# Second mixer of a hybrid encoder: three pieces of queue order moved (keys' output transfers, the last state update, the second band scores)

## The chip, the cores and the metric

The kernel runs on one core of a Trainium2 chip. It is one program in which the five queues (TensorE, VectorE, ScalarE, GpSimd, and SyncE, which issues the weight loads) are written out by hand and meet only through semaphores. The metric is the device time of the whole program in microseconds (us); lower is better. Below, PE is TensorE's matmul side, DVE VectorE, ACT ScalarE, POOL GpSimd.

## What is computed

The reference is a two-layer encoder trunk for 512 prompt tokens and 32 sample tokens that share the weights (544 columns, D_MODEL 1024). Each layer is half a SwiGLU, a mixer, half a SwiGLU. The change lies in the mixer of the second layer, which joins band attention (C) and a Mamba-2 state-space part (D):

```python
bq, bk, bv, z, xbc, dt = jnp.split(h @ w_in, [o1, o2, o3, o4, o5], axis=-1)
bo = band_prompt(bq, bk, bv, rel_bias)              # or band_attend for the sample
new_k, new_v = bk, bv                               # outputs of the step
xbc, conv_new = causal_conv(xbc, conv_buf, conv_w, conv_b)
y, ssm_new = ssd(xs, dt, a, bm, cm, ssm_state)      # chunked recurrence, state is an output
y = rms_norm((y + d_skip * xs) * silu(z), ssd_gain)
return concat(bo, y) @ w_out, new_k, new_v, ssm_new, conv_new
```

All of it is fp32. A large product is made of three fp32r products of high and low halves, so every weight tile is split first into `wh` (high) and `wl` (low) by POOL.

## The kernel before

**Tiles.** The 544 columns are handled as two halves of 272. Activations lie transposed in SBUF (128 features by 544 tokens). The input projection of the mixer is cut into chunks of 128 output features; a chunk has two halves of columns.

**Half products.** `part(n)` on PE (L1492) is half of a chunk: 24 matmuls of 128x272 by `half_product` (L744), into PSUM bank 0 (bank 4 for n = 1). DVE's `part_evac(n)` (L2999, its instruction is at L3009) scales it by the norm and writes it to SBUF. Since nearly all use bank 0, `part(n)` waits for `part_evac(n - 1)`. Parts 0 to 7 give the gates `zs`; parts 8 to 23 the queries `bq_t` and the keys `bk_t` of the band attention. Between two parts PE has the small matmuls of the state-space part (D) and later of the band attention (C), which cover the evacuation. When a chunk is done, POOL splits the next weights (`wh` at L685 from one instruction per half, then `wl` at L689 in pieces of 512).

**State-space part.** For t = 0 to 4 (four prompt tiles, then the sample) DVE does `ssd_sum(t)` (L3060): three instructions make `yn` (L3067, L3069, L3070), then two update the state `sst` (L3072 scales it, both inputs in SBUF; L3075 adds PE's product from bank 6). PE turns `yn` into bank 7 (`ssd_turn`, L1573) and DVE's `ssd_gate(t)` (L3081) multiplies it into `zs`. After the gate of t = 4, ACT squares `zs` in four instructions (L2234), PE sums the squares with 16 matmuls (`ssd_squares`, L1584, which waits for all four), and ACT takes the root (L2237). `sst_ready` reaches 10 with the last state update; the state's output transfer (ACT, L2239) and PE's `band_s(1)` wait for it.

**Band attention.** There are 17 items, (chunk of two heads, tile of 128 queries), three chunks of four tiles, the sample, and the last four tiles. Item n goes through: scores on PE (`band_s`, L1593, matmuls at L1606, banks 2 and 3 for even n, 4 and 5 for odd), bias and minimum on DVE (`band_max`, L3144, at L3156), exponential on ACT (`band_exp`, L2241, at L2247), reciprocal and scaling on DVE (`band_scale`, L3159, at L3165 and L3168, which raises `b_norm`), transposes on PE (`band_turn`, L1621, at L1632, which waits for `b_norm`), a copy on ACT (`band_copy`, L2250, at L2259), and the values' product on PE (`band_out`, L1641, at L1652). The loop on PE runs `band_turn(n)`, a half product, `band_s(n + 2)`, `band_out(n)`. The half product is `part(20 + n)` for n under 4 and one of the output projection after (`ssd_product`, evacuated by `ssd_add`, L3132). ACT's loop runs `band_copy(n)`, `band_exp(n + 2)`, and after n = 3 and n = 5 some DMA issues.

**Order around the change.** PE: `part(16)`, `ssd_out(4)`, `part(17)`, `ssd_turn(4)`, `part(18)`, `ssd_squares`, `band_s(0)`, `band_s(1)`, `part(19)`, then the loop with `band_turn(0)` and `part(20)`. DVE (L3112 to L3116, L3185 to L3190): `part_evac(16)`, `ssd_sum(4)` with the state, `part_evac(17)`, `ssd_gate(4)`, `part_evac(18)`, `band_max(0)`, `band_max(1)`, `band_scale(0)`, `part_evac(19)`, `ssd_inverse` (a reciprocal 544 wide, L3120), then the loop, which begins with `band_scale(1)`.

Of the kernel before, what the change touches and what calls it, by code (L numbers as in the profile page):

```python
# [55 lines left out]
TILES = LP // P  # L56
# [60 lines left out]
def trunk(nc, ins, outs, ret_cdec):  # L117
    with ExitStack() as ctx:
# [101 lines left out]
        bk_t = place("bk_t", [4, T], F32, free_at + 8704)  # L220
# [31 lines left out]
        sst = place("sst", [2, 512], F32, a_at + 4 * SC + 24064)  # L252
# [16 lines left out]
        def bank(b, lo=0, hi=512, r0=0, r1=P):  # L269
            return ps[r0:r1, b, lo:hi]  # L270
# [47 lines left out]
        evac = [sem("evac0"), sem("evac1")]  # L318
# [10 lines left out]
        out_done = sem("out_done")  # L329
# [393 lines left out]
        def _(pe):  # L723
# [768 lines left out]
            def part(n):  # L1492

                m, half = n // 2, n % 2
                s, p_ = chunks[m]
                if n == 0:
                    pe.wait_ge(evac[0], c0 + 4)
                elif n == 2:
                    pe.wait_ge(half_free, HALVES_AB + 1)
                elif half and m:  # L1500
                    pe.wait_ge(half_free, HALVES_AB + m + 1)
                elif m:
                    s_, q_ = chunks[m - 1]
                    pe.wait_ge(evac[s_], (c0, c1)[s_] + q_ + 1)
                half_product(s, (c0, c1)[s] + p_, DC, u, half, 4 if n == 1 else 0)
# [87 lines left out]
            def band_s(n):  # L1593
                c, t = BAND[n]
                B = 2 + 2 * (n % 2)
                if n >= 2:
                    pe.wait_ge(b_max, 2 * (n - 1))
                elif n == 0:
                    pe.wait_ge(seg_exp, 5)
                else:  # L1600
                    pe.wait_ge(sst_ready, 10)
                if t < TILES:
                    w = (t + 1) * P
                    for e in range(2):
                        r = slice(64 * e, 64 * e + 64)
                        last = nc.tensor.matmul(bank(B + e, 0, w), bq_t[r, c, t * P:(t + 1) * P], bk_t[r, c, 0:w],  # L1606
                                                start=True, stop=True)
                else:
                    pe.wait_ge(cdc_loaded, 80)
                    pe.wait_ge(bq_ready, 1)  # L1610
                    for g in range(2):
                        for i in range(2):
                            nc.tensor.matmul(bank(B + g, 0, PAST, 64 * i, 64 * i + 64), bqz[:, 2 * g + i, :, :],
                                             kb_t[:, 2 * g + i, :], start=True, stop=True, skip_group_check=True)
                        for i in range(2):
                            last = nc.tensor.matmul(bank(B + g, PAST, PAST + LS, 64 * i, 64 * i + 64),
                                                    bqz[:, 2 * g + i, :, :], bk_t[:, 2 * g + i, LP:T],
                                                    start=True, stop=True, skip_group_check=True)
                last.then_inc(bs_done, 1)
# [88 lines left out]
            part(18)  # L1708
            ssd_squares()
            band_s(0)  # L1710
            band_s(1)
            part(19)
            for n in range(BAND_N):
                band_turn(n)
                if n and BAND[n - 1][1] == TILES:
# [20 lines left out]
        def _(act):  # L1736
# [529 lines left out]
            for n in range(BAND_N):  # L2266
                band_copy(n)
                if n + 2 < BAND_N:
                    band_exp(n + 2)
                if n == 3:  # L2270
                    act.wait_ge(prod_done[1], c1 + 10)
                    act.dma_start(kb_t[:], ins["kb"]).then_inc(cdc_loaded, 16)
                    act.dma_start(vb_n[:], ins["vb"]).then_inc(cdc_loaded, 16)
                    act.dma_start(bsm[:], ins["bias_s"]).then_inc(cdc_loaded, 16)
                if n == 5:
                    for c in range(4):
                        act.wait_ge(evac[1], c1 + 7 + c)
                        act.dma_start(outs["bk"][c], bk_t[:, c, :]).then_inc(out_done, 16)
            nc.scalar.activation(par[:, P_SPARE:P_SPARE + 1], par[:, P_EPS:P_EPS + 1], ACT.Sqrt)
            squares_after(CD_OUT, 5)  # L2280
            ffn(3, 5)
# [24 lines left out]
        def _(dve):  # L2306
# [384 lines left out]
            def part(n, half):  # L2691

                s, p_ = chunks[n]
                cols_ = slice(half * HT, (half + 1) * HT)
                if p_ == 7:
                    dst, factor = tg[:, s, cols_], 1.0
                    dve.wait_ge(rg_ready, 1 + s)
                elif p_ < 10:
                    dst, factor = sq_t[:, 2 * (p_ - 8) + s, cols_], DH ** -0.5
                else:  # L2700
                    dst, factor = sk_t[:, 2 * (p_ - 10) + s, cols_], 1.0
                if half:
                    dve.wait_ge(prod_done[s], count(p_, s))
                else:
                    dve.wait_ge(half_done, n + 1)
                V.scalar_tensor_tensor(dst, bank(7 - half, 0, HT), factor, rstd[:, cols_], ALU.mult,
                                       ALU.mult).then_inc(evac[s] if half else half_free, 1)
# [291 lines left out]
            def part_evac(n):  # L2999

                m, half = n // 2, n % 2
                s, p_ = chunks[m]
                cols_ = slice(half * HT, (half + 1) * HT)
                dst = zs[:, m, cols_] if m < 4 else (bq_t, bk_t)[m % 2][:, (m - 4) // 2, cols_]
                if half:
                    dve.wait_ge(prod_done[s], count(p_, s))
                else:
                    dve.wait_ge(half_done, HALVES_AB + m + 1)
                V.scalar_tensor_tensor(dst, bank(4 if n == 1 else 0, 0, HT),  # L3009
                                       DH ** -0.5 if m >= 4 and m % 2 == 0 else 1.0, rstd[:, cols_],  # L3010
                                       ALU.mult, ALU.mult).then_inc(evac[s] if half else half_free, 1)
# [48 lines left out]
            def ssd_sum(t):  # L3060

                n = P if t < TILES else LS
                S = sst[:, 0 if t < TILES else 1, :]
                dve.wait_ge(y_done, t + 1)
                if t:
                    dve.wait_ge(yt_done, t)
                link(V.tensor_tensor(head_rows(yn, n), head_rows(bank(4), n), heads(eg[0:n, t % 2, 0:8], n),  # L3067
                                     ALU.mult))
                link(V.tensor_tensor(yn[0:n, :], yn[0:n, :], yt[0:n, :], ALU.add))  # L3069
                V.tensor_tensor(yn[0:n, :], bank(5, 0, 512, 0, n), yn[0:n, :], ALU.add).then_inc(y_sum, 1)  # L3070
                dve.wait_ge(s_scaled, t + 1)
                V.tensor_tensor(head_rows(S), head_rows(S), heads(eg[:, t % 2, 16:24], P),  # L3072
                                ALU.mult).then_inc(sst_ready, 1)
                dve.wait_ge(sst_ready, 2 * t + 1)
                V.tensor_tensor(S, bank(6), S, ALU.add).then_inc(sst_ready, 1)  # L3075
                dve.wait_ge(sst_ready, 2 * t + 2)

            def ssd_gate(t):
                n = P if t < TILES else LS
                dve.wait_ge(yt_done, t + 1)  # L3080
                V.tensor_tensor(zs[:, :, t * P:t * P + n], bank(7).rearrange("p (c r) -> p c r", c=4)[:, :, 0:n],  # L3081
                                zs[:, :, t * P:t * P + n], ALU.mult).then_inc(yz_done, 1)
# [29 lines left out]
            part_evac(16)  # L3112
            ssd_sum(TILES)
            part_evac(17)
            ssd_gate(TILES)
            part_evac(18)  # L3116

# [26 lines left out]
            def band_max(n):  # L3144

                c, t = BAND[n]
                B = 2 + 2 * (n % 2)
                dve.wait_ge(bs_done, n + 1)
                if n == 0:
                    dve.wait_ge(seg_done, 5)  # L3150
                elif n >= 2:
                    dve.wait_ge(bp_done, n - 1)
                w = (t + 1) * P if t < TILES else PAST + LS
                for e in range(2):
                    bias = bt[:, 2 * c + e, (3 - t) * P:512] if t < TILES else bsm[:, e, :]
                    V.tensor_tensor_reduce(pr[n % 2][:, e, 0:w], bank(B + e, 0, w), bias, -1.0, 3e38,  # L3156
                                           ALU.add, ALU.min, bst[:, n % 2, 0, e:e + 1]).then_inc(b_max, 1)
# [26 lines left out]

            dve.wait_ge(bt_masked, 1)  # L3185
            band_max(0)
            band_max(1)
            band_scale(0)
            part_evac(19)
            ssd_inverse()  # L3190
            for n in range(BAND_N):
                if n + 1 < BAND_N:
# [183 lines left out]
```

## Time and profile before

| | |
|---|---|
| median of three runs | 2005.77 us (2005.08 to 2005.82) |
| the profiled execution's own time | 2006.37 us |
| its span in the profile | 2004.6 us |
| PE busy | 1984.9 us |
| DVE, ACT, POOL busy | 1396.2, 1042.7, 1371.8 us |
| mean granted TensorE clock | 0.998 |

The span is first to last instruction; the execution's own time has 1.8 us around it. The mixer's stretch that the change touches lies between 1520 and 1570 us of the span. A row of the timeline gives the start in us, the length in us, engine, line, operation, written tile and read tiles, shapes, the number of merged instructions, and in brackets how long the engine had been idle before and what ended that.

### The profile page before, as it was taken

The numbers are of one execution on the slowest core, as the hardware profiler recorded it, in microseconds if no ns is written. First come the engines' busy times: TensorE is split into PE (matmuls) and PEld (weight loads), VectorE is DVE, ScalarE is ACT, GpSimd is POOL, SyncE is SP. The second block draws the span as 40 slices with busy tenths as digits, with TensorE's granted clock in tenths as the row PEclk, the third lists the DMA queues.
The fourth block names the chain that finished last, engine by engine and source line by source line (L and its number), as shares of the span: only waits on it lengthen the run. The fifth ranks groups of instructions, "written<-read, shape, count | busy, mean of one in ns | idle before, by whom it ended". The sixth has DMA issues, their size and how long they took to land.

```text
span 2004.6 us, 42159 instructions
## 1 busy us (share of the span) xinstructions
PE 1984.9 (99%) x16036; PEld 1942.6 (97%) x16036; DVE 1396.2 (70%) x2282; ACT 1042.7 (52%) x2045; POOL 1371.8 (68%) x1126
## 2 busy tenths in 40 slices
PE   9999999999999999999999999999999999999998
PEld 8999999999989999999999999999998799999997
DVE  7877766524857886876778677665976678768664
ACT  6766754221344665665357566532432437656651
POOL 6978866654425887986779788665643269878764
PEclk9999999999999999999999999999999999999999
DMA  4322322231212222222223222233210222322322
GB/s 161 108 93 98 106 106 104 88 107 64 79 45 90 91 106 104 87 106 101 90 85 106 106 103 91 104 121 115 91 64 33 92 95 96 106 98 93 106 96 77
DMA packets 34031, 190.92 MB, mean 95 GB/s; under 512 B 4144, under 2 KB 6704, under 8 KB 15408
## 3 DMA queue, kind: packets, MB, share of 16 engines
q1 hardware_dynamic: 26496, 173.43, 24.7%
q10 hardware_dynamic: 7344, 14.89, 2.1%
q8 instruction: 127, 2.08, 0.4%
q14 instruction: 64, 0.52, 0.1%
HBM read 180.81 MB, written 7.50 MB: 94 GB/s over the span
## 4 chain that ended last, share of the span: by engine, by line
PE 94%; DVE 3%; POOL 1%; ACT 1%; issue 1%; DMA 0%; ACTq 0%; POOLq 0%; SPq 0%; DVEq 0%
PE ps L821 59%; PE ps L736 16%; PE ps L751 9%; PE ps L1053 2%; DVE u L2328 1%; PE ps L897 1%; PE ps L1606 1%; POOL wl L689 1%; PE ps L1652 0%; PE ps L1309 0%; PE ps L1301 0%; PE ps L1257 0%; PE ps L1632 0%; PE ps L1568 0%; PE ps L1075 0%
## 5 line engine op out<-in xcount | busy, mean ns | idle before, releaser
L821 PE MATMUL ps<-tt,ws 128*128 128x272 f32 x3840 | 523.0, 289 | 1.6 <-issue 1.6
L821 PEld LDWEIGHTS ps<-tt,ws 128*128 128x128 f32 x3840 | 497.9, 188 | 2.9 <-issue 2.4
L602 POOL TENSOR_TENSOR ws<-wraw,ws 128x512 fp32r<-128x512 f32 x336 | 433.8, 1305 | 40.0 <-ACT ws L1864 24.5
L602 POOL TENSOR_TENSOR ws<-s,ws 128x512 fp32r<-128x512 f32 x224 | 291.5, 1301 | 197.0 <-ACT ws L1902 137.7
L821 PE MATMUL ps<-u,ws 128*128 128x272 f32 x2880 | 400.4, 288 | 0.0
L821 PEld LDWEIGHTS ps<-u,ws 128*128 128x128 f32 x2880 | 376.6, 188 | 0.2
L685 POOL TENSOR_SCALAR wh<-wraw 128x1024 fp32r<-128x1024 f32 (+2 forms) x116 | 108.9, 939 | 351.0 <-PE ps L751 207.2
L689 POOL TENSOR_TENSOR wl<-wraw,wh 128x512 fp32r<-128x512 f32 (+1 forms) x207 | 281.4, 1377 | 9.7
L2497 DVE TENSOR_TENSOR s<-ps,wraw 128x512 f32<-128x512 f32 x112 | 77.5, 692 | 189.0 <-POOL ws L602 189.0
L821 PE MATMUL ps<-ta,ws 128*128 128x272 f32 x1536 | 207.3, 287 | 0.0
L821 PEld LDWEIGHTS ps<-ta,ws 128*128 128x128 f32 x1536 | 198.1, 188 | 0.0
L736 PE MATMUL ps<-u,wh 128*128 128x272 f32 x1120 | 187.7, 289 | 1.5 <-DVE tg L2380 0.9
L736 PEld LDWEIGHTS ps<-u,wh 128*128 128x128 f32 x1120 | 156.7, 188 | 4.0 <-issue 2.4
L821 PE MATMUL ps<-a,ws 128*128 128x272 f32 x1152 | 160.4, 288 | 0.0
L821 PEld LDWEIGHTS ps<-a,ws 128*128 128x128 f32 x1152 | 150.7, 188 | 0.0
L751 PE MATMUL ps<-u,wh 128*128 128x272 f32 x704 | 137.4, 293 | 0.7 <-DVE bq_t L3009 0.4
L1912 ACT COPY snap<-ps 128x272 f32<-128x272 f32 x112 | 43.2, 386 | 148.8 <-PE ps L821 148.7
L2466 DVE TENSOR_TENSOR a<-tg,a 128x544 fp32r<-128x544 f32 x88 | 117.1, 1331 | 2.9 <-ACT a L1842 2.9
L736 PE MATMUL ps<-u,wl 128*128 128x272 f32 x560 | 115.4, 287 | 0.0
L751 PEld LDWEIGHTS ps<-u,wh 128*128 128x128 f32 x704 | 110.6, 188 | 3.5 <-issue 1.2
L1936 ACT ACTIVATE ps<-tg 128x544 f32<-128x544 f32 x80 | 50.3, 629 | 115.8 <-DVE tg L2548 59.1
L736 PE MATMUL ps<-a,wh 128*128 128x272 f32 x616 | 101.8, 287 | 0.0
(415 smaller groups left out, 3860.4 us busy)
## 6 DMA issues: line engine op xcount, KB each, us to landing
wraw<-in_wf_in SPq DMA_DIRECT2D x87, 1024.0 KB, 4.8
wraw<-in_wf_out SPq DMA_DIRECT2D x32, 1024.0 KB, 4.8
wraw<-in_wf_out SPq DMA_DIRECT2D x16, 768.0 KB, 4.2
wraw<-in_w_ab SPq DMA_DIRECT2D x12, 1024.0 KB, 4.8
wraw<-in_w_cd SPq DMA_DIRECT2D x10, 1024.0 KB, 4.8
wraw<-in_w_abo SPq DMA_DIRECT2D x8, 512.0 KB, 3.2
wraw<-in_w_cdo SPq DMA_DIRECT2D x8, 512.0 KB, 3.4
wraw<-in_w_bv SPq DMA_DIRECT2D x2, 1024.0 KB, 5.5
```

What stands on the lines that cost most here:

```text
L602: return nc.gpsimd.tensor_tensor(wide(p, b, 1), src, wide(p, b, 0).bitcast(F32), ALU.subtract)
L685: nc.gpsimd.tensor_scalar(highs[:, to], raw, 1.0, 1.0, ALU.mult, ALU.mult).then_inc(w_high, 1)
L689: piece = nc.gpsimd.tensor_tensor(lows[:, some], wraw[:, par_, s * K * P + some.start: s * K * P + some.stop], highs[:, some].bitcast(F32) ...
L736: last = nc.tensor.matmul(bank(b0 + 2 * s + half, 0, HT), w[:, k * P:(k + 1) * P], act_t[:, k0 + k, part, half * HT:(half + 1) * HT], star ...
L751: last = nc.tensor.matmul(bank(b, 0, HT), w[:, s, k * P:(k + 1) * P], act_t[:, k, part, half * HT:(half + 1) * HT], start=(k == 0 and w is ...
L821: last = nc.tensor.matmul(bank(b, 0, HT), ws[weights][w][:, i * P:(i + 1) * P], moving[:, part], start=(start and i == 0 and w == 0 and pa ...
L897: last = nc.tensor.matmul(bank(half, 0, HT), w[:, 0, k * P:(k + 1) * P], u[:, k, part, half * HT:(half + 1) * HT], start=(k == 0 and w is ...
L1053: last = nc.tensor.matmul(bank(2 * s + half, 0, HT), w[:, s, k * P:(k + 1) * P], a[:, k, part, half * HT:(half + 1) * HT], start=(k == 0 a ...
L1912: nc.scalar.copy(snap2[:], bank(X_BANK[p.b], 0, HT)).then_inc(snap_ready, 1)
L1936: nc.scalar.activation(pair(GATE_PAIR[p.b]), halves(tg[:, 0, :]), ACT.Silu).then_inc(sil_done, 1)
L2466: V.tensor_tensor(a[:, slot(i), 1, :], tg[:, 1 + i % 2, :], a[:, slot(i), 0, :].bitcast(F32), ALU.subtract).then_inc(act_ready, 1)
L2497: V.tensor_tensor(s34[:, 1, 0:n], bank(S2_BANK, 0, n), quarter(p, 1), ALU.add).then_inc(w_sum, 1)
```

## The change

Three edits. (1) ACT issued all four transfers of the keys to `out_bk` after item 5; now it issues one after each of items 5, 6, 7 and 8. (2) `ssd_sum` is cut in two: `ssd_state` holds the two state instructions. For the prompt tiles nothing moves; for the sample they come behind `part_evac(17)`, and still ahead of `ssd_gate(4)`. (3) On PE `part(19)` goes ahead of `band_s(1)`, and on DVE `part_evac(19)` ahead of `band_max(1)` and so ahead of `band_scale(0)`.

```diff
             ssd_squares()
             band_s(0)
+            part(19)
             band_s(1)
-            part(19)
             for n in range(BAND_N):
                 band_turn(n)
...
-                if n == 5:
-                    for c in range(4):
-                        act.wait_ge(evac[1], c1 + 7 + c)
-                        act.dma_start(outs["bk"][c], bk_t[:, c, :]).then_inc(out_done, 16)
+                if 5 <= n < 9:
+                    act.wait_ge(evac[1], c1 + 2 + n)
+                    act.dma_start(outs["bk"][n - 5], bk_t[:, n - 5, :]).then_inc(out_done, 16)
...
             def ssd_sum(t):
...
                 V.tensor_tensor(yn[0:n, :], bank(5, 0, 512, 0, n), yn[0:n, :], ALU.add).then_inc(y_sum, 1)
+                if t < TILES:
+                    ssd_state(t)
+
+            def ssd_state(t):
+                S = sst[:, 0 if t < TILES else 1, :]
                 dve.wait_ge(s_scaled, t + 1)
                 V.tensor_tensor(head_rows(S), head_rows(S), heads(eg[:, t % 2, 16:24], P),
                                 ALU.mult).then_inc(sst_ready, 1)
...
             ssd_sum(TILES)
             part_evac(17)
+            ssd_state(TILES)
             ssd_gate(TILES)
             part_evac(18)
...
             dve.wait_ge(bt_masked, 1)
             band_max(0)
+            part_evac(19)
             band_max(1)
             band_scale(0)
-            part_evac(19)
             ssd_inverse()
```

## Rows read from the trace of the kernel before

**Rows 1.** The page's first part: busy time, share of the span, instructions.

```profile
PE 1984.9 (99%) x16036; PEld 1942.6 (97%) x16036; DVE 1396.2 (70%) x2282; ACT 1042.7 (52%) x2045; POOL 1371.8 (68%) x1126
```

**Rows 2.** Timeline, from the last state update to the sum of squares.

```profile
1522.07 0.67 DVE L3072 TENSOR_TENSOR sst<-sst,eg 128x512 f32<-128x512 f32 x1
...
1522.93 0.28 PE L751 MATMUL ps<-u,wl 128*128 128x272 f32 x1
...
1523.39 1.05 POOL L685 TENSOR_SCALAR wh<-wraw 128x1024 fp32r<-128x1024 f32 x1 [6.14 <-PE ps L751]
1523.50 0.44 DVE L3009 SCALAR_TENSOR_TENSOR bq_t<-ps,rstd 128x272 f32<-128x272 f32 x1
1523.86 0.28 DVE L3081 TENSOR_TENSOR zs<-ps,zs 128x128 f32<-128x128 f32 x1
...
1524.00 0.52 PE L751 MATMUL ps<-u,wh 128*128 128x272 f32 x2 [0.42 <-DVE bq_t L3009]
1524.17 2.30 ACT L2234 ACTIVATE yq<-zs 128x544 f32<-128x544 f32 x4 [13.67 <-DVE zs L3081]
...
1524.52 2.55 POOL L689 TENSOR_TENSOR wl<-wraw,wh 128x512 fp32r<-128x512 f32 x2
...
1527.11 3.83 PE L1588 MATMUL ps<-yq,const 128*128 128x272 f32 x16
```

**Rows 3.** Timeline, the first band items and part 19.

```profile
1530.87 0.93 PE L1606 MATMUL ps<-bk_t,bq_t 64*128 64x128 f32 x8
...
1533.92 0.17 DVE L3165 RECIPROCAL bst<-bst 128x2 f32<-128x2 f32 x1 [1.21 <-ACT pr L2247]
...
1534.12 0.48 DVE L3168 TENSOR_SCALAR pr<-pr,bst 128x128 f32<-128x128 f32 x2
...
1534.87 0.38 PE L1632 MATMUL ps<-const,pr 128*128 128x128 f32 x2
1535.07 0.44 DVE L3009 SCALAR_TENSOR_TENSOR bk_t<-ps,rstd 128x272 f32<-128x272 f32 x1 [0.47 <-PE ps L751]
...
1535.57 0.52 PE L751 MATMUL ps<-u,wh 128*128 128x272 f32 x2 [0.31 <-DVE bk_t L3009]
```

**Rows 4.** Timeline, band scores 128 and 256 wide behind a half product.

```profile
1549.06 0.49 PE L1606 MATMUL ps<-bk_t,bq_t 64*128 64x128 f32 x4
...
1549.17 0.44 DVE L3009 SCALAR_TENSOR_TENSOR bk_t<-ps,rstd 128x272 f32<-128x272 f32 x1
...
1549.48 0.88 PE L1652 MATMUL ps<-pt,bv_n 128*64 128x128 f32 x12
...
1571.39 0.70 PE L1606 MATMUL ps<-bk_t,bq_t 64*128 64x256 f32 x4
...
1572.14 0.42 DVE L3156 CUSTOM_DVE_ANT_0 pr<-ps,bt 128x256 f32<-128x256 f32 x1 [0.20 <-PE ps L1606]
```

**Rows 5.** Timeline, a state scaling and an item scaling beside POOL's split.

```profile
1506.45 1.79 POOL L689 TENSOR_TENSOR wl<-wraw,wh 128x512 fp32r<-128x512 f32 x1
...
1507.73 1.05 DVE L3072 TENSOR_TENSOR sst<-sst,eg 128x512 f32<-128x512 f32 x1
...
1569.55 0.62 POOL L685 TENSOR_SCALAR wh<-wraw 128x512 fp32r<-128x512 f32 x1 [5.99 <-PE ps L751]
...
1569.66 0.59 DVE L3168 TENSOR_SCALAR pr<-pr,bst 128x128 f32<-128x128 f32 x1
```

**Rows 6.** The keys' transfer line (length in ns, min/median/max; first, last start), then timeline.

```profile
L2278 ACTq DMA_DIRECT2D out_bk<-bk_t x4: 350/450/467, 1563.7 to 1565.1; - x4
...
1565.64 0.80 ACT L2259 COPY pt<-ps 128x768 f32<-128x768 f32 x1 [1.03 <-issue]
...
1566.49 0.88 PE L1652 MATMUL ps<-pt,bv_n 128*64 128x128 f32 x12 [0.86 <-ACT pt L2259]
```

**Rows 7.** Stretches near the end: length, busy PE, PEld, DVE, ACT, POOL, granted clock, DMA.

```profile
1992.00:1996.00 4.00, 1.52 (x13) 0.70 (x13) 3.18 (x8) 1.03 (x3) 0.00 (x0) 1.00 0.10 33
1996.00:2000.00 4.00, 2.18 (x4) 1.18 (x4) 3.97 (x10) 0.39 (x1) 0.28 (x1) 0.60 0.68 238
```

More of the change, by code:

```diff
@@ L3062, in ssd_sum @@
                 n = P if t < TILES else LS
-                S = sst[:, 0 if t < TILES else 1, :]
                 dve.wait_ge(y_done, t + 1)
```

## The prediction

> **What bounds the kernel now.** I read the page's busy shares first, then the list of who waited for whom on PE, then the timeline around each of the waits that the change can touch. PE is busy for 99% of the span [rows 1], so time is only won by closing a gap on PE, and lost by opening one; what the other engines do counts only where PE waits for it. In the mixer's stretch three gaps stand: 0.42 us before `part(18)`, which waits for `part_evac(17)` [rows 2]; 0.31 us before `part(20)`, which waits for `part_evac(19)` [rows 3]; and 0.86 us before `band_out(6)`, which waits for ACT's copy [rows 6]. Together 1.59 us, under 0.08% of the kernel. About 0.2% (4.0 us) is what a measurement can tell from no change here. So the three edits can't win anything that is seen; the question is whether they open new gaps.
>
> **Edit 1, the transfers.** The fourth issue starts at 1565.1 and with up to 0.47 us of length the queue is free near 1565.54; the copy of item 6 starts at 1565.64 although ACT had been idle for 1.03 us, that is from 1564.61 [rows 6]. With one issue (0.35 us from 1563.7) the queue is free at 1564.05, under the exponentials. The copy then starts near 1564.70, ends near 1565.50, and PE, free at 1566.49 - 0.86 = 1565.63, doesn't wait. That is worth the whole gap, **-0.86**. The other three issues land behind `band_exp(8)`, `(9)` and `(10)`, each at most 0.47 us, hidden by the exponentials before them and by the half product for which PE has work anyway; unhidden, they would cost 0.47 each. The transfers themselves go later by some items, and nothing in the mixer waits for them. Bounds: 0 (another thing holds the copy) to -0.86.
>
> **Edit 2, the state update.** The two state instructions take from 1522.07 to 1523.50, 1.43 us, and the last matmul of `part(17)` ends at 1522.93 + 0.28 = 1523.21 [rows 2]. With them gone from in front, `part_evac(17)` starts at about 1523.25, ends 0.44 later at 1523.69, and `part(18)` starts 0.06 after it (as 1523.94 to 1524.00 before) at 1523.75: 0.25 earlier. But the pair now stands ahead of `ssd_gate(4)`, and behind the gate hang ACT's four squares and, behind all four, PE's `ssd_squares`. Before, the squares ended at 1524.17 + 2.30 = 1526.47 and PE came at 1527.11: 0.64 of slack [rows 2], and PE now comes at 1526.86. The chain: the pair starts at 1523.62 (the next instruction starts some 0.08 before the evacuation ends, as the gate did). Undisturbed, it takes its 1.43, the gate starts at 1525.05, ACT 0.31 after (1523.86 to 1524.17 before), ends 2.30 later at 1527.66, PE starts at 1527.72: +0.61 against 1527.11. That is the lower bound.
>
> It will not be undisturbed. POOL's `wh` split runs from 1523.39 to 1524.44 [rows 2], released by the same product. When the same state scaling met POOL at 1507.73 it took 1.05 instead of 0.67 and ended 0.54 after POOL's instruction did (1508.78 against 1508.24) [rows 5]. So here it ends at 1524.44 + 0.54 = 1524.98 instead of 1524.29; the rest of the pair takes 1.43 - 0.67 = 0.76, the gate starts at 1525.74, ACT at 1526.05, ends at 1528.35, PE starts at 1528.41: **+1.30**, the value that I take, since it is the same instruction against the same engine. The adding half reads PSUM and I cost it as before.
>
> The Trainium skill (SBUF — State Buffer, Who interferes with whom) says that a VectorE instruction with two SBUF inputs and a GpSimd one that reads SBUF exclude each other, and that the second waits until the first is over. By its letter the scaling would run its full 0.67 after POOL's end, and the sum below would be 0.13 larger; the row, with 0.54, says that part of the instruction runs before, and I go by the row.
>
> **Edit 3, the second scores.** What it takes away: `part(20)` no longer waits for bank 0, since `band_s(1)` stands between. What it adds is larger. `band_scale(0)` is now behind `band_max(1)`, which needs `band_s(1)`, which is behind all of `part(19)`; and `band_turn(0)`, PE's very next work, waits for `band_scale(0)`. I count from the start e of `part_evac(19)`, before at 1535.07, with `part(20)` at e + 0.50 [rows 3].
> First, e itself moves: the joint scores took 0.93 less the usual overlap of 0.07, 0.86 [rows 3]; a single 128-wide one holds PE for 0.42 (1549.06 to 1549.48) [rows 4]. So e comes 0.44 earlier after `ssd_squares`: **-0.44**.
> Then: `band_s(1)` starts at e - 0.11 (1549.06 against 1549.17), DVE's first 256-wide minimum 0.75 after that (1571.39 to 1572.14), two of 0.42 less overlap, 0.69 [rows 4], so the reciprocal starts at e + 1.33, the scaling 0.20 later at e + 1.53, and lasts 0.48: e + 2.01. Then 0.06 to PE and 0.39 for the transposes (1534.87 to 1535.57 - 0.31) [rows 3]: `part(20)` at e + 2.46, that is +1.96. This is the lower bound.
> POOL again: its split of the next weights starts 0.14 after e (1523.39 against 1523.25 for the same event), `wh` lasts 1.05, and the two `wl` pieces, 0.08 later, 1.28 each [rows 2]: pieces from e + 1.27 to 2.54 and to 3.82. The scaling meets the first. When a 128-wide scaling met POOL at 1569.66 it took 0.59 and ended 0.08 after POOL's 1570.17 [rows 5], where half of the pair of 0.48 is 0.24. So the first half ends at e + 2.62. The second either slips through (e + 2.82, `part(20)` at e + 3.27, +2.77) or loses to the second piece (e + 3.95, `part(20)` at e + 4.40, +3.90), the upper bound. Both starts fall within 0.1 us, so this is a toss-up; I take the middle, **+2.77**, nearest to the row with two scalings in a row. The norm's long reciprocal and `part_evac(20)` shift with the scaling by less than PE does, so nothing new is late in the loop.
>
> **Sum** against the profiled execution (2006.37, which is 0.60 above the median): +1.30 - 0.44 + 2.77 - 0.86 = +2.77, so 2009.1 for a profiled one, and on the median 2005.77 + 2.77 = **2008.5**. Bounds: +0.61 - 0.44 + 1.96 - 0.86 = +1.3 and +1.30 - 0.44 + 3.90 - 0.86 = +3.9.
>
> **Rivals.**
> (a) POOL doesn't disturb either of the two places: +1.3, 2007.0. For it: POOL's start may fall elsewhere by a few tenths. Against: rows 5. 0.18.
> (b) The second half of the scaling loses to POOL's second piece: +3.9, 2009.7. 0.20.
> (c) Edit 1 saves nothing, because the copy is held by something else than the issues: +3.6, 2009.4. The idle 1.03 "issue" speaks against it. 0.08.
> (d) Only the savings count: something lets the squares and the first scaling come in time. -0.25 - 0.31 - 0.86, with 0.19 for the scores taken apart (0.42 + 0.63 against 0.86, the 0.63 being 0.70 less overlap): -1.2, 2004.5. It would need a semaphore that I misread; 0.07.
> (e) Slower beyond doubt: TensorE's clock falls. Place: the new gap before `band_turn(0)`, 1.5 to 3.4 us. In the trace the clock was 1.00 in 1992 to 1996 with PE busy for 1.52 of 4.0 us and 0.60 in the stretch after [rows 7], that is partly at the 1.2 GHz level. If that follows here, `part(20)` takes up to twice as long; `part(18)` held PE for 3.1 us (1524.00 to 1527.11) [rows 2], so +3.1: 2.8 + 3.1 = +5.9, 2011.7. It decides only if PE is as idle here as it was there. 0.07. The Trainium skill (TensorE: Matmul & The Clock Gate, Why this matters for your kernels) speaks against opening gaps between bursts of matmuls for this reason; rows 7 agree that it happens after a nearly idle stretch.
>
> **How the numbers follow.** Forecast 0.38, (a) 0.18, (b) 0.20, (c) 0.08, (d) 0.07, (e) 0.07, something unseen 0.02. Range: from (a) less the spread of the runs, 0.4, that is 2006.6, to (b) plus the 0.13 and 0.4, that is 2010.2; it leaves out (d) and (e). Slower by over 0.2% needs +4.0: all of (e), a quarter of (b): 0.12. Faster by over 0.2% is out of reach of 1.59 us; 0.01. Within 0.2%: 0.87.
>
> **What would show it.** Edit 1 right: the copy of item 6 no longer shows "issue", no PE wait at L1652. Edit 2: PE's 0.42 before `part(18)` falls to about 0.17, and a new PE wait at L1588 for ACT `yq` of 1.5 us (0.9 if POOL leaves it alone); the state scaling 1.3 us long. Edit 3: no PE wait for `bk_t`, a new one at L1632 for DVE `pr` of 1.5 to 3.4 us, with a scaling of over 0.5 us. If PE shows neither new wait, the forecast is wrong; if both and the time is lower, the gaps were closed again later.

## The result and the profile after

| | before | changed |
|---|---|---|
| median | 2005.63 us (10 runs, 2004.57 to 2007.33) | 2010.4 us (10 runs, 2009.84 to 2011.54) |
| ratio, 95% interval | | 1.0025 [1.0017, 1.0033] |
| span of the profiled execution | 2004.6 us | 2008.5 us |
| mean granted TensorE clock | 0.998 | 0.997 |

The change makes the kernel 4.8 us slower, clear of noise: above the 2008.5 that I forecast and just above the range's end of 2010.2.

The execution that was profiled reached the mixer 0.9 us earlier than that of before (POOL's split behind part 17 starts at 1522.46 against 1523.39 [rows 2]), so absolute starts of the two traces differ by that. To compare traces I use a stretch of PE alone, from the last matmul of `ssd_out(4)` (L1568) to the last band score (L1606); the third number of a row below is where they start.

Before, the view of one line (lengths in ns as min/median/max; first and last start in us), PE:

```profile
L1568 PE MATMUL ps<-xd,seg x80: 214/275/275, 1458.5 to 1519.8; 128*128 128x64 f32 x64, 32*32 32x64 f32 x16
...
L1606 PE MATMUL ps<-bk_t,bq_t x64: 272/481/693, 1530.9 to 1599.9; 64*128 64x128 f32 x16, 64*128 64x256 f32 x16, 64*128 64x384 f32 x16, 64*128 64x512 f32 x16
```

Changed, the same view:

```profile
L1568 PE MATMUL ps<-xd,seg x80: 214/275/275, 1457.6 to 1518.8; 128*128 128x64 f32 x64, 32*32 32x64 f32 x16
...
L1606 PE MATMUL ps<-bk_t,bq_t x64: 272/481/693, 1531.3 to 1603.8; 64*128 64x128 f32 x16, 64*128 64x256 f32 x16, 64*128 64x384 f32 x16, 64*128 64x512 f32 x16
```

80.1 us before, 85.0 after: +4.9, so the whole loss arises here. The spans differ by only 3.9, since the changed kernel's profiled execution came to this place 0.9 earlier; behind the last band score both have 404.7 us left, so nothing is given back later. The changed kernel's list of who waited for whom on PE in the mixer (us in total, times, longest):

```profile
PE ps L1632 <- DVE pr L3172: 3.3, 1, 3.3
PE ps L1588 <- ACT yq L2234: 1.4, 1, 1.4
PE ps L751 <- DVE bq_t L3008: 0.2, 1, 0.2
```

The waits of 0.31 [rows 3] and 0.86 [rows 6] are gone and the 0.42 [rows 2] is 0.2, as the edits mean to; two new ones stand in their place. First, edit 2 in the timeline of the changed kernel:

```profile
1522.31 0.44 DVE L3008 SCALAR_TENSOR_TENSOR bq_t<-ps,rstd 128x272 f32<-128x272 f32 x1 [1.11 <-PE ps L751]
...
1522.46 1.04 POOL L685 TENSOR_SCALAR wh<-wraw 128x1024 fp32r<-128x1024 f32 x1 [6.14 <-PE ps L751]
1522.67 1.37 DVE L3075 TENSOR_TENSOR sst<-sst,eg 128x512 f32<-128x512 f32 x1
1522.81 0.52 PE L751 MATMUL ps<-u,wh 128*128 128x272 f32 x2 [0.17 <-DVE bq_t L3008]
...
1524.80 0.29 DVE L3084 TENSOR_TENSOR zs<-ps,zs 128x128 f32<-128x128 f32 x1
...
1525.12 2.30 ACT L2234 ACTIVATE yq<-zs 128x544 f32<-128x544 f32 x4 [15.56 <-DVE zs L3084]
...
1527.47 3.93 PE L1588 MATMUL ps<-yq,const 128*128 128x272 f32 x16 [1.38 <-ACT yq L2234]
```

The state scaling (now L3075) is 1.37 us long instead of 0.67, the gate (L3084) waits behind it, and PE finds the squares unfinished. Against POOL's split, which starts on the same product in both traces, `ssd_squares` starts after 5.01 us (1522.46 to 1527.47) instead of 3.72 [rows 2]: +1.29.

Then edit 3, the timeline of the changed kernel around `part_evac(19)`; narrow windows keep the two scalings and POOL's two pieces apart:

```profile
1534.97 0.70 PE L1606 MATMUL ps<-bk_t,bq_t 64*128 64x256 f32 x4
...
1535.07 0.44 DVE L3008 SCALAR_TENSOR_TENSOR bk_t<-ps,rstd 128x272 f32<-128x272 f32 x1 [2.58 <-PE ps L751]
...
1536.34 1.26 POOL L689 TENSOR_TENSOR wl<-wraw,wh 128x512 fp32r<-128x512 f32 x1
...
1536.61 1.08 DVE L3172 TENSOR_SCALAR pr<-pr,bst 128x128 f32<-128x128 f32 x1
...
1537.57 1.26 POOL L689 TENSOR_TENSOR wl<-wraw,wh 128x512 fp32r<-128x512 f32 x1
...
1537.61 1.30 DVE L3172 TENSOR_SCALAR pr<-pr,bst 128x128 f32<-128x128 f32 x1
...
1538.96 0.69 PE L1632 MATMUL ps<-const,pr 128*128 128x128 f32 x2 [3.29 <-DVE pr L3172]
...
1543.64 0.92 PE L1606 MATMUL ps<-bk_t,bq_t 64*128 64x384 f32 x4
```

The first scaling ends at 1537.69, 0.09 after POOL's first piece; the second at 1538.91, 0.08 after the second piece. Together 2.30 us for what takes 0.48 alone [rows 3]. The stretches around it (length; busy PE, PEld, DVE, ACT, POOL with counts; granted clock; DMA):

```profile
1531.50:1535.50 4.00, 4.00 (x32) 3.50 (x32) 0.94 (x5) 2.82 (x6) 0.28 (x1) 1.00 0.32 131
1535.50:1539.50 4.00, 0.71 (x5) 0.54 (x4) 3.76 (x9) 1.09 (x4) 3.24 (x3) 0.87 0.00 0
1539.50:1543.50 4.00, 4.00 (x25) 3.99 (x24) 3.65 (x4) 0.37 (x1) 0.00 (x0) 0.70 0.43 135
```

PE did 0.71 us of work in 4.0, and the clock fell: 0.87 and 0.70 are mixes of full speed (2.4 GHz) and half of it. In stretches of half a microsecond the clock reads 0.96 from 1538.0 to 1538.5, so the fall comes while PE still waits, 0.50 from there to 1541.5, 0.63 in the next one, and 1.00 again from 1542.0. The transposes last 0.69 instead of 0.38 [rows 3], and from their start to the next scores (part 20 between) it is 4.68 us. Within part 20 the rate comes back; two rows of its timeline, the same pair of matmuls:

```profile
1540.81 0.66 PE L751 MATMUL ps<-u,wh 128*128 128x272 f32 x2
...
1542.42 0.41 PE L751 MATMUL ps<-u,wh 128*128 128x272 f32 x2
```

### The profile page after: what moved, and what is told of

Read it like the earlier page. It is cut to its first block, busy times and chain, and to the rows that moved or that the text cites. A ratio compares the mean times of both kernels' runs of the same rounds, so it can differ in the third digit from the quotient of the medians.

```text
span 2008.5 us, 42159 instructions
## 1 busy us (share of the span) xinstructions
PE 1985.7 (99%) x16036; PEld 1943.3 (97%) x16036; DVE 1399.1 (70%) x2282; ACT 1042.6 (52%) x2045; POOL 1370.2 (68%) x1126
## 4 chain that ended last, share of the span: by engine, by line
PE 94%; DVE 3%; POOL 1%; ACT 1%; issue 1%; DMA 0%; POOLq 0%; SPq 0%; DVEq 0%; ACTq 0%
PE ps L821 59%; PE ps L736 16%; PE ps L751 9%; PE ps L1053 2%; PE ps L897 1%; PE ps L1606 1%; DVE u L2327 1%; POOL wl L689 1%; PE ps L1652 1%; PE ps L1632 0%; PE ps L1309 0%; PE ps L1301 0%; PE ps L1257 0%; PE ps L1568 0%; PE ps L1075 0%
```

## The experiments

Theory: three costs, each with its place: +1.3 (edit 2: state ahead of the gate, lengthened by POOL), over 3 (edit 3: the scaling behind the second scores, lengthened by POOL twice), over 1 (the clock), against -0.9 (edit 1). The rivals: PE's own order costs; the gap is order alone and POOL is innocent; the clock falls only where two gaps come together.

The stretch of PE, the PE waits within it, and the median (the kernel before had 2005.4 to 2005.5 beside all of these):

| kernel | stretch us | against 80.1 | its new or remaining PE waits | median us |
|---|---|---|---|---|
| edit 1 alone | 79.2 | -0.9 | 0.4, 0.3 | 2003.96 |
| edit 2 alone | 81.5 | +1.4 | 1.4, 0.9, 0.3, 0.2 | 2007.15 |
| edit 3 alone | 83.2 | +3.1 | 3.3, 0.9, 0.4 | 2010.1 |
| changed, first scaling early | 81.0 | +0.9 | 1.4, 0.6, 0.2 | 2006.23 |
| changed, gate ahead of state | 83.5 | +3.4 | 3.3, 0.2 | 2008.58 |
| changed, scaling on ACT | 82.0 | +1.9 | 1.7, 1.4, 0.2 | 2007.97 |
| changed, filler matmuls | 83.7 | +3.6 | 1.4, 0.2 | 2009.45 |
| changed, both repairs | 79.3 | -0.8 | 0.6, 0.2 | 2004.69 |
| edit 1, gate first, edit 3 undone | 78.8 | -1.3 | 0.3, 0.2, 0.2 | 2004.28 |

**Each edit alone.** The edit 1 kernel is the one before with the `5 <= n < 9` lines of the diff.

> The kernel before with edit 1 alone (one transfer of the keys after each of the items 5 to 8). Theory: the four issues held ACT's copy of item 6, so the PE wait of 0.86 us at the values' product disappears and no new one comes; time -0.9 us against before, within noise of it (2004.8). Rival: the copy was held by something else, and the wait stays; 0.0. Second rival: the three later issues each hold a copy; +0.5 to +1.4 and new PE waits at the values' product.

Measured: -0.9 in the stretch; by time it can't be told from no change, ratio 0.9995 [0.9986, 1.0004]; no wait at the values' product. The timeline of this kernel's ACT:

```profile
1564.84 0.35 ACTq L2277 DMA_DIRECT2D out_bk<-bk_t  x1
...
1565.55 0.18 ACT L2247 ACTIVATION_READ_ACCUMULATOR pr<-pr,bst 128x1 f32 x1
1565.64 0.78 ACT L2259 COPY pt<-ps 128x768 f32<-128x768 f32 x1
```

One issue is over at 1565.19, under the exponential, and the copy follows 0.09 after the start of ACT's read-out instead of 1.03 after its end [rows 6].

> The kernel before with edit 2 alone (sample's state update behind part_evac(17), still ahead of the gate). Theory: the wait of 0.42 us before part(18) falls to 0.17 and PE gets a wait of 1.4 us at the sum of squares for ACT's squares; the state scaling lasts 1.37 us instead of 0.67 since POOL's weight split runs; PE reaches the sum of squares 1.3 us later than before and the time is +1.3 us. Clock 1.00 throughout. Rival: the mixer takes it up again (a later gap closes), and the time is that of before: then a PE wait behind the sum of squares must be gone that stands in before.

Measured: stretch +1.4, ratio 1.0009 [1.0000, 1.0018]. The state scaling lasts 1.36 us, the wait is 1.38:

```profile
1523.34 1.36 DVE L3076 TENSOR_TENSOR sst<-sst,eg 128x512 f32<-128x512 f32 x1
...
1528.13 3.93 PE L1588 MATMUL ps<-yq,const 128*128 128x272 f32 x16 [1.38 <-ACT yq L2234]
```

Nothing takes it up: the 0.9 and the 0.3 of before are there too. That POOL's split is what lengthens the scaling is read from where it ends: in the changed kernel at 1524.04, 0.54 behind POOL's instruction (1522.46 + 1.04), as forecast from [rows 5]. No run takes POOL away at this place.

> The kernel before with edit 3 alone (part 19 ahead of the second scores, on DVE its evacuation ahead of the second minimum and of the first scaling). Theory: a PE wait of 3.3 us ahead of the first transposes, two scalings of 2.3 us together, the granted clock well under 1 in the 4 us after, part(20) about 4 us long instead of 3.2; the wait of 0.31 before part(20) gone, that of 0.86 at item 6 still there; time +4.5 us (2010.1). Rival: the clock falls only because edit 2 has put another gap of 1.4 us some 10 us ahead; then the clock stays at 1.00 here and the time is +3.4.

The wait came (3.29), the price of the whole too by its median: ratio 1.0025 [1.0016, 1.0035]. But the profiled execution had its clock at 1.00 throughout: stretch +3.1, and its own time was 2009.09, the lowest of ten, 1.0 under the median. The other nine had a mean granted clock of 0.997 or 0.996, this one 0.998. From its timeline, item 0 at full clock:

```profile
1534.22 0.44 DVE L3009 SCALAR_TENSOR_TENSOR bk_t<-ps,rstd 128x272 f32<-128x272 f32 x1 [2.58 <-PE ps L751]
...
1535.75 2.30 DVE L3168 TENSOR_SCALAR pr<-pr,bst 128x128 f32<-128x128 f32 x2
...
1538.11 0.44 PE L1632 MATMUL ps<-const,pr 128*128 128x128 f32 x2 [3.29 <-DVE pr L3168]
...
1541.49 0.92 PE L1606 MATMUL ps<-bk_t,bq_t 64*128 64x384 f32 x4
```

POOL holds the scalings just as long as in the changed kernel, without edit 2. A second trace of the same kernel:

> Edit 3 alone once more, for a second trace; in the first the clock stayed at 1.00 through the gap of 3.3 us while its median run was 1.0 us longer than the run that was profiled. Theory: the gap is at the edge, where the same kernel falls in some executions and not in others; most fall, so most likely 0.6 to 0.7 in the 4 us after the gap and a turn of 0.7 us. Rival: without edit 2 the clock never falls, and the trace looks like the first.

Here too the execution with the trace kept the clock (2009.07 us, clock 1.00 in every stretch of 4 us from 1527.5 to 1543.5, PE's stretch 83.2). So neither trace shows the fall for this kernel; the nine lower means speak for it, without a place. What the two traces do show is the price of edit 3 at full clock, +3.1.

**Which part of edit 3.** DVE's order alone is put back in this one; PE's stays as changed:

```diff
             band_max(0)
+            band_scale(0)
             part_evac(19)
             band_max(1)
-            band_scale(0)
```

> The changed kernel with DVE's order put to band_max(0), band_scale(0), part_evac(19), band_max(1); PE's order stays as changed. Theory (the scaling behind the second scores is what costs): the PE wait of 3.3 us ahead of the first transposes is gone and with it the low clock; since the long reciprocal now starts about 1 us later against part(20), a new small wait of about 0.4 us comes at the transposes of item 1 or before part(21). Against the kernel before: +1.3 (edit 2) -0.4 +0.4 +0.4 -0.9 = +0.8, and -4 us against the changed kernel. Rival: PE's order itself costs (scores apart, bank 0); then part(20) is still over 2 us later than in before.

Stretch +0.9, ratio 1.0005 [0.9996, 1.0014]. The 3.3 and the low clock are gone; the scaling, now beside part 19 with POOL idle, takes 0.48. A wait of 0.59 stands at the transposes of item 1 behind the long reciprocal, as expected in place and near it in size:

```profile
1535.22 0.48 DVE L3172 TENSOR_SCALAR pr<-pr,bst 128x128 f32<-128x128 f32 x2
...
1541.53 0.66 PE L1632 MATMUL ps<-const,pr 128*128 128x128 f32 x4 [0.59 <-DVE pr L3172]
```

So PE's order is not what costs the 3.3; DVE's is.

**Order or POOL.** ACT does item 0's two scalings (`nc.scalar.activation(pr[0][:, e, 0:P], ..., ACT.Copy, scale=bst[:, 0, 2, e:e + 1])`) between its exponentials for items 0 and 1, DVE only the small reciprocal.

> The changed kernel with the two scalings of item 0 done by ACT instead of DVE (ahead of item 1's exponentials); the order on PE stays. ACT has no port in common with POOL. Theory (of the 3.3 us, 1.4 is the order and 1.9 is POOL holding DVE's scaling): the wait ahead of the first transposes is 1.4 to 1.8 us, about 0.4 each for ACT's two scalings. If the clock falls from the length of the gap, it stays at 1.00 and the time is 1.6 + 1.1 = 2.7 us under the changed kernel. Rival: the wait is all order, ACT's scalings end as late as DVE's did, and the gap stays over 3 us. Rival on the clock: it falls with the shorter gap too, and 1.1 us of the gain is missing.

The timeline of this kernel, with POOL's split at the same place:

```profile
1535.79 2.52 POOL L689 TENSOR_TENSOR wl<-wraw,wh 128x512 fp32r<-128x512 f32 x2
...
1536.05 0.69 ACT L2267 ACTIVATE pr<-pr,bst 128x128 f32<-128x128 f32 x2 [2.27 <-DVE bst L3174]
...
1536.80 0.44 PE L1632 MATMUL ps<-const,pr 128*128 128x128 f32 x2 [1.68 <-ACT pr L2267]
```

The wait is 1.68 instead of 3.29 with POOL's pieces as long as ever, so at least 1.6 us of edit 3 are POOL and the rest is order. (ACT's pair of scalings takes 0.69 where DVE's takes 0.48 alone; by DVE's lengths POOL's share is 2.30 - 0.48 = 1.8.) In the trace the clock stayed at 1.00; yet 5 of the 10 runs had a mean clock of 0.997 with a median of 2008.3, the other 5 had 0.998 and 2006.8. The kernel before had 0.997 in 4 of 33. Whether this shorter gap is the place where those five lost it, no trace shows.

**The clock by itself.** 24 matmuls on PE behind the second scores, results unused:

```diff
             part(19)
             band_s(1)
+            for i in range(24):
+                nc.tensor.matmul(bank(1, 0, HT), u[:, 0, 0, 0:P], u[:, 1, 0, 0:HT], start=True, stop=True,
+                                 skip_group_check=True)
```

> The changed kernel with 24 matmuls of 128x272 put on PE behind the second scores, into a bank that nobody reads before it is written anew; they last about 3.0 us and fill the gap of 3.3 us. Their results are not used. Theory (the low clock is a cost of its own, 1.1 us): the granted clock stays at 1.00 through 1535 to 1545, the first transposes take 0.4 instead of 0.7 us and part(20) 3.2 instead of 4.0, the scaling ends as late as before, and the time is 1.1 us under the changed kernel. Rival: part(20) is long for another reason (weights, POOL), and the time is the same or, with the fillers, longer.

```profile
1536.06 3.28 PE L1714 MATMUL ps<-u 128*128 128x272 f32 x24
...
1537.07 2.36 DVE L3175 TENSOR_SCALAR pr<-pr,bst 128x128 f32<-128x128 f32 x2
...
1539.48 0.44 PE L1632 MATMUL ps<-const,pr 128*128 128x128 f32 x2
...
1542.87 0.92 PE L1606 MATMUL ps<-bk_t,bq_t 64*128 64x384 f32 x4
```

The scaling is as late as ever, and PE does useless work through the gap; from the transposes to the next scores it is now 3.39 us instead of 4.68, and the stretch is 83.7 instead of 85.0. All ten runs have a mean clock of 0.998. So the low clock costs 1.3 us in the trace, and no more than that hangs on it; the median is 1.0 us under the changed kernel's 2010.4. Twice the changed kernel:

> The changed kernel once more, for a second trace. Theory: PE's wait ahead of the first transposes is 3.3 us again (it is set by the order and by POOL's two pieces), and the clock falls again, part(20) 3.6 to 4.2 us long. Rival: the clock fell by chance in the one trace; then it is 1.00 here, and part(20) 3.0 us.

2011.05 us, wait 3.30, the granted clock in the two stretches behind:

```profile
1535.50:1539.50 4.00, 0.75 (x5) 0.30 (x4) 3.61 (x9) 1.09 (x4) 3.54 (x3) 1.00 0.00 0
1539.50:1543.50 4.00, 3.95 (x20) 3.95 (x21) 3.93 (x4) 0.37 (x1) 0.00 (x0) 0.57 0.43 135
```

It fell again, later against the work: this trace runs 0.6 us behind the first one here (the transposes start at 1539.55), and in stretches of half a microsecond the clock reads 1.00 up to 1539.5, 0.74 in the next one and 0.50 from 1540.0 to 1543.0. Transposes to scores take 4.91 us.

**Repairs.** The gate goes ahead of the state. Since the sum of squares writes the bank from which the state update reads, PE must wait for the state too:

```diff
             part_evac(17)
-            ssd_state(TILES)
             ssd_gate(TILES)
+            ssd_state(TILES)
...
                 pe.wait_ge(y_sq, 4)
+                pe.wait_ge(sst_ready, 10)
```

> The changed kernel with the sample's gate ahead of its state update on DVE; since PE's sum of squares writes the bank that the state update reads, PE waits there for the state too. Theory: the gate starts 0.1 us after the evacuation, ACT's squares end 2 us earlier than in the changed kernel, and the PE wait of 1.4 us at the sum of squares is gone, the state's end being 1 us before PE gets there; 1.4 us faster than the changed kernel, +3.4 against before. The wait of 3.3 us ahead of the first transposes stays. Rival: the state's end takes the place of the squares, and a wait of some 0.1 to 1 us stays.

Stretch 83.5, 1.5 under the changed kernel, median 2008.58, ratio to before 1.0016 [1.0007, 1.0025]; no wait at the squares. This kernel has no gap of 1.4 ahead, and its clock fell all the same in the trace (0.63 in the stretch of 4 us from 1535.5, in which the gap of 3.3 ends at 1536.70), which speaks against the rival that it takes two gaps. Its trace also bears on edit 2: the state scaling, now behind the gate, starts 0.43 us into POOL's split, is 1.16 long and ends at 1523.41, again 0.54 behind POOL's instruction (1521.82 + 1.05). Its end goes with POOL's end and not with its own start.

> The changed kernel with both repairs together: the gate ahead of the state update (PE's sum of squares waits for the state), and the first scaling ahead of part_evac(19) and of the second minimum. Theory: no wait at the sum of squares, none of 3.3 us, none of 0.86; against before -0.25 (part 18 earlier) -0.44 (joint scores behind) +0.41 (scores apart) +0.4 (reciprocal later against part 20) -0.86 = -0.75 us, 2004.9. Rival: the reciprocal costs over 1 us at item 1, and the kernel is no faster than before.

Stretch -0.8, ratio 0.9996 [0.9987, 1.0005], as expected; the wait behind the reciprocal is 0.61.

> The kernel before with edit 1, the state update behind part_evac(17) and behind the gate (PE's sum of squares waits for the state), and edit 3 undone. Theory: only savings are left, 0.25 before part 18 and 0.86 at item 6; from the last ssd_out matmul to the last band score PE takes 79.0 us (80.1 in before, 79.3 with the first scaling moved up and edit 3 kept), time -1.1 us against before, 2004.4. The wait of 0.3 before part(20) stays. Rival: edit 3 repaired is worth as much as undone, and this is 0.3 us slower than the kernel with both repairs.

Stretch 78.8, -1.3, the shortest of all; ratio 0.9995 [0.9986, 1.0004]. A wait of 0.2 at item 6 stays beside the 0.3. By the traces it beats the kernel before and the changed one, and it is 0.5 us shorter than the kernel with both repairs, so edit 3 doesn't pay even when repaired. The timing can't tell it from the kernel before.

## Why the prediction failed

**What held.** The direction of each step, the two places of the new waits, and edit 1 and edit 2 to 0.1 us: -0.86 forecast and -0.9 measured; +1.30 and +1.29, with the state scaling forecast to end 0.54 after POOL, length 1.36, measured 1.37. There the Trainium skill's letter (SBUF — State Buffer, Who interferes with whom) would have given 0.13 more; the row was nearer. `part_evac(19)` comes 7.60 us after the squares' first matmul instead of 7.96, -0.36 for the -0.44.

**The step that failed, first half.** "The second either slips through (...) or loses to the second piece (...). Both starts fall within 0.1 us, so this is a toss-up; I take the middle, +2.77, nearest to the row with two scalings in a row." It lost, in every trace of a kernel with this order: five kernels or repeats besides the changed one show the wait of 3.3 or, with fillers, two scalings of 2.36. The row I leaned on [rows 5] shows its first scaling only; here are the pair and POOL's next instruction, from the kernel before:

```profile
1569.66 0.78 DVE L3168 TENSOR_SCALAR pr<-pr,bst 128x128 f32<-128x128 f32 x2
...
1570.25 1.33 POOL L689 TENSOR_TENSOR wl<-wraw,wh 128x512 fp32r<-128x512 f32 x1
```

POOL's `wh` ends there at 1570.17 and its `wl` begins 0.08 later, and the pair was through at 1570.44. In the changed kernel the second piece begins at 1537.57, before the first scaling ends at 1537.69. I read it so that the second scaling slips through in the free moment between two POOL instructions and finds none between pieces that follow at once; the rows agree, but no run varied that distance. The words were also off by themselves: of two branches held to be a toss-up, +2.77 is the lower one and not the middle, and (b) was given 0.20 against 0.38. The first scaling ended at e + 2.62 as forecast, the second at e + 3.84 (e + 3.95 for the case (b)). From e to the next scores it is 7.27 us in edit 3 alone (1534.22 to 1541.49) against 3.71 in before (from 1535.07 [rows 3] to the scores below): +3.56 at full clock.

```profile
1538.78 0.92 PE L1606 MATMUL ps<-bk_t,bq_t 64*128 64x384 f32 x4
```

So the upper bound of +3.90 was the right branch, and I took 0.8 too little. It was 0.3 too high: by 0.11 in the scaling's end (I let it end 0.13 behind the piece, where the row had 0.08), and by 0.19 in the transposes, behind which part 20 starts after 0.20 in edit 3 alone (1538.11 to 1538.31) and not after 0.39.

**The step that failed, second half.** The clock was rival (e), at 0.07 and apart from (b), though its place was named rightly. But the two hang together: the branch that makes the gap 3.3 us is the one in which PE is as idle as in the stretch before the clock fell near the end [rows 7], 0.71 of 4.0 here against 1.52 there. Even that reading was too coarse: in the kernel before, PE had no work at all from 1995.0 to 1996.5, and the clock reads 1.00 to 1996.5, 0.81 to 1997.0 and 0.50 from there, so there too it fell at the end of a gap and not in a stretch of thin work. Once (b) had a fair chance, (e) had to be costed behind it. Its price was off the other way: +3.1 forecast, 1.3 measured (1.5 in the second trace), for the half rate lasts only until somewhere within part 20 and not to its end.

**The sum as it is.** +1.29 - 0.36 + 3.56 + 1.3 - 0.86 = +4.9, the stretch's +4.9. By experiments: +1.4 (edit 2) + 3.1 (edit 3 at full clock) + 1.3 (clock) - 0.9 (edit 1) = +4.9. The range left out exactly the joint case, (b) with (e) at the price measured here.

## What to carry to other kernels

Before an instruction is moved on one queue, list what is queued behind its new place and which of it the busiest engine will want next: both losses came from work that was not yet awaited (a state update, an evacuation and the second scores) set ahead of work that was awaited at once. In these traces a short VectorE instruction beside GpSimd pieces that follow one another at once cost nearly a whole piece each time (1.08 and 1.30 us for 0.24), so a few of them must be priced one by one. And a gap on TensorE can have a second price in the clock (1.3 to 1.5 us here behind a gap of 3.3); where one rival makes the gap and another lives off it, cost them together.

## What was not expected of the hardware

A scaling of 128 columns (0.24 us alone, half of the pair of 0.48) was 1.08 and then 1.30 us long, and one scaling ended behind each of POOL's pieces, by 0.09 and 0.08 us. The second scaling began just 0.04 us after POOL's second piece (1537.61 and 1537.57) and was held for all of it. The state scaling, 0.67 us alone, ended 0.54 us behind POOL's instruction in each of three places, whatever its own start. The clock fell in both traces of the changed kernel and in neither of edit 3 alone, with the same gap of 3.3 us and the same work behind it; the fall began some 0.5 us before the transposes in one and 0.2 us after their start in the other, and cost 1.3 and 1.5 us (from `part_evac(19)` to the next scores, 8.57 and 8.80 us against the 7.27 at full clock). The likely reason for the difference is that low time within the gap costs PE nothing. With the gate first the fall came about 0.2 us before the transposes and cost 1.5 (8.73 us). What decides in which execution it falls, the runs don't show.
